# A stick-breaking attention's inner loop: 64-row score products, a merged late sum, one activation table set

## What is computed

```python
SB_HEADS = 16          # head dimension 64
def _sb_block(q_blk, k, v, q_pos):
    t_len = k.shape[2]
    k_pos = jnp.arange(t_len)
    z = jnp.einsum('bhqd,bhkd->bhqk', q_blk, k).astype(jnp.float32) * (SB_HEAD_DIM ** -0.5)
    causal = k_pos[None, :] < q_pos[:, None]
    log_keep = jnp.where(causal, -jax.nn.softplus(z), 0.0)
    after = lax.cumsum(log_keep, axis=3, reverse=True) - log_keep
    w = jnp.where(causal, jnp.exp(jax.nn.log_sigmoid(z) + after), 0.0)
    return jnp.einsum('bhqk,bhkd->bhqd', w.astype(v.dtype), v)
```

## Time and profile before

| | |
|---|---|
| runs | 1962.29, 1963.96, 1966.81 us |
| median | 1963.96 us |
| profiled execution, its own time | 1960.74 us |
| its span | 1959.0 us |
| TensorE passes, busy | 1829.1 us (93%) |
| VectorE busy | 514.5 us (26%) |
| ScalarE busy | 274.9 us (14%) |
| GpSimd busy | 115.6 us (6%) |
| chain that ended last | PE 62%, DMA 31%, DVE 4%, ACT 1%, POOL 1% |
| mean granted TensorE clock | 0.984 |

### The profile page before, as it was taken

How to read it: one execution, slowest core, us unless ns; L and a number is a source line. 1 busy time by engine, 2 the same in 40 slices (tenths; PEclk the granted TensorE clock), 3 DMA queues, 4 the chain that set the end, 5 groups by cost and what they waited for, 6 DMA issues and landing times.

```text
span 1959.0 us, 21688 instructions
## 1 busy us (share of the span) xinstructions
PE 1829.1 (93%) x8558; PEld 1051.4 (54%) x8559; DVE 514.5 (26%) x1047; ACT 274.9 (14%) x537; POOL 115.6 (6%) x151
## 2 busy tenths in 40 slices
PE   5997899999999899899899898989999999999998
PEld 3445733333333233233233234877888888788887
DVE  1136533232222222222222223123110005611000
ACT  1024311100010000000000002026110002311000
POOL 4003600000000000000000002000000000100000
PEclk7998999999999999999999999999999999899999
DMA  9684299979999999999999997420343343343430
GB/s 353 257 257 130 75 380 428 428 307 428 429 428 428 428 428 428 428 428 428 429 428 428 429 429 285 152 106 1 129 166 134 129 160 119 129 172 129 172 129 22
DMA packets 93092, 547.38 MB, mean 279 GB/s; under 512 B 5906, under 2 KB 9186, under 8 KB 65298
## 3 DMA queue, kind: packets, MB, share of 16 engines
q1 hardware_dynamic: 90864, 544.33, 68.8%
q10 hardware_dynamic: 2178, 2.34, 0.4%
HBM read 545.60 MB, written 1.05 MB: 279 GB/s over the span
## 4 chain that ended last, share of the span: by engine, by line
PE 62%; DMA 31%; DVE 4%; issue 1%; ACT 1%; POOL 1%; SPq 0%; ACTq 0%; DVEq 0%; POOLq 0%
DMA ring<-in_exp_w 30%; PE ps L1092 20%; PE ps L1192 12%; PE ps L1032 11%; PE ps L726 4%; PE ps L1063 4%; PE ps L912 1%; DMA ring<-in_ada_w 1%; PE ps L986 1%; PE ps L1004 1%; PE ps L1227 1%; PE ps L687 1%; PE ps L1144 1%; DVE arena L1998 1%; PE ps L814 0%
## 5 line engine op out<-in xcount | busy, mean ns | idle before, releaser
L1032 PE MATMUL ps<-ring,arena 128*64 128x512 f32 x2112 | 474.0, 596 | 56.3 <-DMA ring<-in_exp_w 56.2
L1092 PE MATMUL ps<-hn,ring 128*128 128x272 f32 (+1 forms) x1536 | 348.6, 390 | 0.0
L1032 PEld LDWEIGHTS ps<-ring,arena 128*64 128x64 f32 x2112 | 148.3, 137 | 362.3 <-issue 240.5
L1092 PEld LDWEIGHTS ps<-hn,ring 128*128 128x128 f32 x1536 | 293.9, 191 | 53.5
L1063 PE MATMUL ps<-arena 128*64 128x512 f32 x1056 | 233.9, 595 | 3.5
L1192 PE MATMUL ps<-arena,ring 128*128 128x272 f32 (+1 forms) x1024 | 228.5, 386 | 1.1 <-DVE arena L1948 1.1
L1192 PEld LDWEIGHTS ps<-arena,ring 128*128 128x128 f32 x1024 | 194.7, 190 | 34.6 <-DVE arena L1948 1.9
L1063 PEld LDWEIGHTS ps<-arena 128*64 128x64 f32 x1056 | 75.2, 137 | 140.8 <-issue 140.6
L1273 ACT ACTIVATE arena<-ps 128x512 f32<-128x512 f32 (+2 forms) x135 | 71.0, 534 | 403.7 <-PE ps L1063 212.2
L1845 DVE TENSOR_SCALAR arena<-ps 128x512 f32<-128x512 f32 x33 | 22.8, 692 | 364.6 <-PE ps L1032 364.6
L1758 DVE TENSOR_SCALAR arena<-arena,rstd 128x64 f32<-128x64 f32 x68 | 18.3, 312 | 304.3 <-PE ps L1032 303.6
(11 more groups left out here) (375 smaller groups left out, 1273.8 us busy)
## 6 DMA issues: line engine op xcount, KB each, us to landing
ring<-in_exp_w SPq DMA_DIRECT2D x128, 2048.0 KB, 24.7
arena<-in_exp_w SPq DMA_DIRECT2D x64, 2048.0 KB, 21.8
ring<-in_mlp_w_up SPq DMA_DIRECT2D x16, 2048.0 KB, 7.6
ring<-in_mlp_w_down SPq DMA_DIRECT2D x16, 2048.0 KB, 7.6
ring<-in_ada_w SPq DMA_DIRECT2D x12, 2048.0 KB, 13.1
ring<-in_sb_w_qkv SPq DMA_DIRECT2D x6, 2048.0 KB, 14.0
ring<-in_w_in SPq DMA_DIRECT2D x5, 2048.0 KB, 10.0
ring<-in_lru_w_in SPq DMA_DIRECT2D x4, 2048.0 KB, 7.8
```

What stands on the lines that cost most here:

```text
L1032: last = mm(bank(2 + part)[64 * h:64 * h + 64, :], lhs, w[:, k % 2, at:at + 512], start=False, stop=(k == C - 1))
L1092: last = mm(bank((n0 + q) % 8)[:, lo:TT], w[:, k, P * q:P * q + P], act[:, k, lo:TT], start=(k == 0), stop=(k == C - 1))
```

## The change

Four edits. `bk` loses its plane per head: a block's keys stand in one plane, head 0 in rows 0 to 63 and head 1 in rows 64 to 127, evicted by one instruction per chunk; the zeroing of it and VectorE's wait for it go. `b_score` sends both masks first and then, part by part, the product of head 0 on rows 0 to 63 and that of head 1 on rows 64 to 127. `b_accumulate` has one product instead of L1146 and L1147, whose output are the two groups of 16 columns and whose input reads the 16 columns twice. ScalarE loads the set `natural_log_exp_and_others` once, ahead of the eight blocks.

```diff
@@ -325,7 +325,7 @@
 
         a = Area(arena)
         self.bq = a.take(C, TT)
-        self.bk = a.take(C, 2, TT)
+        self.bk = a.take(C, TT)
         self.bv = a.take(C, TT)
         self.vtok = a.take(3, D)
         self.bO = a.take(C, TT)
@@ -600,7 +600,6 @@
         part = m.bmask[:, at:at + n]
         link(g.affine_select(out=part, in_=part, pattern=[[1, n]], compare_op=ALU.is_gt, fill=NEG,
                              base=0, channel_multiplier=-1))
-    link(g.memset(m.bk, 0.0))
     link(g.memset(m.vtok[:, 2, :], 0.0))
     g.memset(m.za[:, 0, 0, 0:1], 0.0).then_inc(s["b_consts"], 1)
 
@@ -1126,15 +1125,14 @@
 
     def b_score(i):
 
+        outs = [bank(2 * (i % 3) + h) for h in range(2)]
+        rows = (slice(0, 64), slice(64, P))
         for h in range(2):
-            out = bank(2 * (i % 3) + h)
-            mm(out[:, 0:432], m.identb, m.bmask, start=True, stop=False, skip_group_check=True)
-            mm(out[:, 0:TT], m.bk[:, i, h, 0:P], m.bq[:, i, :], start=False, stop=False,
-               skip_group_check=True)
-            mm(out[:, TT:416], m.bk[:, i, h, P:2 * P], m.bq[:, i, P:TT], start=False, stop=False,
-               skip_group_check=True)
-            last = mm(out[0:META, 416:432], m.bk[:, i, h, 2 * P:TT], m.bq[:, i, 2 * P:TT],
-                      start=False, stop=False, skip_group_check=True)
+            mm(outs[h][:, 0:432], m.identb, m.bmask, start=True, stop=False, skip_group_check=True)
+        for k0, keys, at in ((0, P, 0), (P, P, TT), (2 * P, META, 416)):
+            for h in range(2):
+                last = mm(outs[h][0:keys, at:at + TT - k0], m.bk[rows[h], i, k0:k0 + keys], m.bq[rows[h], i, k0:TT],
+                          start=False, stop=False, skip_group_check=True)
         last.then_inc(s["b_scored"], 1)
 
     def b_accumulate(i):
@@ -1143,8 +1141,8 @@
             out, sp = bank(2 * (i % 3) + h), m.sp[:, i % 2, h, :]
             mm(out[:, 0:432], m.lower, sp, start=False, stop=False, skip_group_check=True)
             mm(out[:, P:TT], m.mones, sp[:, TT:416], start=False, stop=False, skip_group_check=True)
-            mm(out[:, 256:TT], m.mones, sp[:, 416:432], start=False, stop=False, skip_group_check=True)
-            last = mm(out[:, 400:416], m.mones, sp[:, 416:432], start=False, stop=True,
+            late = out[:, P:416].rearrange("p (b n) -> p b n", b=2)[:, :, P:TT - P]
+            last = mm(late, m.mones, sp[:, 416:432].unsqueeze(1).to_broadcast([P, 2, META]), start=False, stop=True,
                       skip_group_check=True)
         last.then_inc(s["b_summed"], 1)
 
@@ -1451,6 +1449,7 @@
         act.wait_ge(s["b_exp"], i + 1)
         f(m.za[:, i % 3], m.za[:, i % 3], ACT.Ln, bias=m.ones[:, 0:1]).then_inc(s["b_ln"], 1)
 
+    nc.scalar.preload_act_table_set("natural_log_exp_and_others")
     soft(0)
     soft(1)
     for i in range(8):
@@ -1890,14 +1889,10 @@
     for n in range(24):
         dve.wait_ge(s["chunk_done"], n + 1)
         src = bank(n % 8)[:, 0:TT]
-        if n == 8:
-            dve.wait_ge(s["b_consts"], 1)
         if n < 8:
             last = v.scalar_tensor_tensor(m.bq[:, n, :], src, DH ** -0.5, m.rstd[:], ALU.mult, ALU.mult)
         elif n < 16:
-            for h in range(2):
-                rows = slice(64 * h, 64 * h + 64)
-                last = v.tensor_tensor(m.bk[rows, n - 8, h, :], src[rows, :], m.rstd[rows, :], ALU.mult)
+            last = v.tensor_tensor(m.bk[:, n - 8, :], src, m.rstd[:], ALU.mult)
         else:
             last = v.tensor_tensor(m.bv[:, n - 16, :], src, m.rstd[:], ALU.mult)
         last.then_inc(s["chunk_dve"], 1)
```

## The result

| | before | changed |
|---|---|---|
| median | 1964.05 us (1962.29 to 1966.81, 4 runs) | 1944.61 us (1941.89 to 1946.08, 4 runs) |
| profiled execution | 1960.74 us | 1941.89 us |
| its span | 1959.0 us | 1940.1 us |

The ratio is 0.9908, with a 95% interval of 0.9895 to 0.9921. So the change saved 17.6 to 19.4 us by the medians; 17.2 were forecast, and a median of 1946.8 us.

The account below looks back on a forecast made before the run. TensorE or the expert weights' DMA was taken to carry nearly all of the chain. Savings of 3.78 (memset), 2.65 (clock) and 10.79 (attention) made 17.2 us, from 1963.96 to 1946.8 us, range 1942.5 to 1951.0.

Parts of the forecast that it names:

- The memset: Second block's first norm: without zeroing bk TensorE waits 3.78 us less; no half clock behind it saves 2.65 more.
- Row groups: Attention scores: paired 64-row products overlap, so b_score takes 1.52 us for 2.28, about 0.75 less per block.
- Late sums: b_accumulate: one product replaces two, saving 0.22 us per head, 0.43 per block.
- Table set: Attention on ScalarE: 16 of 17 loads go; chain from score to sum 4.33 us for 5.59, TensorE stays the bound.
- The attention summed up: Second block's attention: entry, iterations 0 to 6 and last sum together 10.79 us less.
- The clock at the entry: Attention entry: TensorE's gap shrinks from 3.25 to 2.8 us, and the half clock behind it was left in.
- no overlap: Rival, attention scores: row groups run one after another, score 2.46 us, gain 10.2 us, 1953.7 us; chance 0.10.
- the chain as bound: Rival, attention: ScalarE and VectorE bind, iterations up to 5.59 us, gain 11.5 us, 1952.5 us; chance 0.07.
- the lasting half clock: Rival, attention: clock stays at 1.2 GHz, iteration about 9.9 us, about 17 us slower, 1981 us; chance 0.03.
- No fall at the entry: Rival, attention entry: the clock dip goes too, gain 18.8 us, 1945.2 us; chance 0.30.

Follow-up runs that it names:

- b2_table_only: Kernel before with only the single table set loaded ahead of the eight blocks; median 1956.49 against 1961.38 us.
- b3_late_only: Kernel before with only the late sums merged into one product; median 1956.99 against 1961.38 us.
- b4_rows_only: Kernel before with only the scores in two row groups, zeroing of bk kept; median 1960.42 against 1961.38 us.
- c2_rows_and_table: Kernel before with row groups and one table set, zeroing and separate late sums kept; median 1952.68 against 1961.75 us.
- a1_head_by_head: Changed kernel with all three 64-row products of head 0, then all three of head 1; median 1953.67 against 1961.52 us for the kernel before.
- c4_fill_recurrence: Changed kernel plus 6 idle products ahead of the recurrence's output projection; median 1941.49 against 1944.20 us for the changed kernel.
- a3_squares_first: Changed kernel with GpSimd's sum of the first norm's squares ahead of its attention constants; median 1940.82 against 1961.52 us for the kernel before.
- c1_changed_again: The changed kernel unaltered, timed again; median 1944.20 against 1961.75 us for the kernel before.
- a4_zero_planes: Changed kernel with the old zero-plane scores and evictions, zeroing behind the norm's sum; median 1946.79 against 1961.52 us for the kernel before.
- b1_memset_late: Kernel before with bk and vtok zeroed behind the first norm's sum of squares, nothing removed; median 1954.37 against 1961.38 us.
- c3_best: Changed kernel with squares' sum first, 13 mask products at the attention's entry, 6 idle products before the recurrence's projection; median 1939.35 against 1944.20 us.

## Why the prediction was right

The median came out at 1944.61 us for 1946.8, and the mechanism is the one forecast: each step below was read in its own place.

*The memset* (-3.78 and -2.65). Right in place and size: 6.40 us measured up to the first mask, and moving the zeroing alone brings more than that back. The second term is less sure than it was written. The 6.8 us at half clock were one profile's. In `b2_table_only`, `b3_late_only`, `b4_rows_only` and `c2_rows_and_table`, with waits of 4.91 to 4.94 us, it lasted 3.4 us, and the stretch to the first mask was 102.2 to 102.3 us for 103.2. So the term is 1.6 to 2.65, by the execution, and that this step came out to the tenth was luck in part.

*Row groups* (1.52 per score). Measured 1.52. Both halves of the argument held: the overlap read off L1004, and 0.20 for the change of shape. The head-by-head run shows that the overlap was the gain (without it a score took 2.55, for 2.46 in the rival's sum), and the run with row groups alone that the other parts had to make room for it.

*Late sums* (-0.43). Measured 0.44 alone.

*Table set* (chain 5.59 to 4.33). Measured 4.32. The guess of 0.05 us between exponential and logarithm was 0.03. That TensorE stays the bound was right, with a loop beside the chain that the prediction did not have: the one through VectorE's order, some 4.4 us here. With the loads in place it was this loop (5.69) that decided.

*The attention summed up* (-10.79). Measured 10.81: first sum 5.85 us behind the first mask, iteration 0 of 5.60, five of 4.95, 4.32 before the last sum.

*The clock at the entry.* The forecast left the fall in, and it was there in both profiles of this kernel. But its reasoning, by the length of the gap, does not hold: the same gap of 2.73 us had a fall in `c4_fill_recurrence` and none in `a3_squares_first` and `c2_rows_and_table`. That the 10.79 us came out as 10.81 was luck in this term, which is worth 1.7 us.

*What was not forecast.* 1.4 us of the profiled difference lie in the recurrence, where the half clock lasted 10.2 us in one profile and 3.4 in the other; the change has no part in that stage.

The rivals: no overlap would have shown a score of about 2.5 us, the chain as bound an idle time before each sum, the lasting half clock an iteration near 9.9. None was there. No fall at the entry, the first rival, is what `a3_squares_first` had in the same stage.

## What to carry to other kernels

Products on half the rows cost what full ones do; the gain is in the pair, so put the two row groups next to each other in the program's order, here in different banks (one bank for both was not tried). Before costing a faster step, follow every loop through the other engines' own orders, not only the chain of one block: row groups alone gave almost nothing until the table loads were out of such a loop. And look for set-up work on an idle engine ahead of a sum that the bound engine waits for: its place alone was worth 5 to 7 us here, by how long the clock stays down behind the wait.

## What the runs showed of the hardware

A wait of TensorE is often followed by a stretch at 1.2 GHz, and the length of the wait does not settle it. The waits in the second block, by length:

| wait | half clock with it |
|---|---|
| 4.91 to 4.94 us, 4.01 us, 3.25 us | in every profile |
| 2.73 us | in `after`, `c1_changed_again` and `c4_fill_recurrence`; none in `a3_squares_first` and `c2_rows_and_table` |
| 2.11 us | 6.8 us in `b2_table_only`, 3.4 in `a1_head_by_head`; none in `a4_zero_planes` |
| 2.09 and 1.75 us | in `b3_late_only` and `b4_rows_only` |
| 1.66 us | none in `before` and `b1_memset_late` |
| 1.58 us and 1.68 us | none in any profile |

Here `before` and `after` are the profiles of the two kernels. The fall starts during the wait or up to 1.5 us behind its end, except in the recurrence of `b1_memset_late`, where two shorter waits come between. Where idle products fill most of the 3.25 us (`c4_fill_recurrence`, `c3_best`), the fall comes behind waits of 0.50, 1.13 and 1.43 us. The stretches last 3.4, 6.8 or 10.2 us. At the norm and at the entry 3.4 us of it cost 1.4 to 1.7 us and 6.8 us of it 2.6 to 3.1, as much as a step of this change and different from one execution to the next. In the recurrence 10.2 us cost only 1.3 to 2.2 us more than 3.4: TensorE waits for VectorE there in between, and less so at the half clock (1.01 us in the changed kernel's profile, 0.62 in the one before). What decides whether the clock falls behind waits of 1.7 to 2.8 us stays open.
